# A third buffer for queries and decays, and turns of 13 pieces with the low-rank products in two parts

## The chip, the cores and the metric

The kernel runs on one core of a Trainium2 chip. The metric is the device time of one execution in microseconds. Before the change it is 1311.18 us, the median of three runs (1310.85 to 1312.26).

## What is computed

One encoder layer on 256 tokens of width 2048: a norm, an input projection, three mixers side by side (neighbourhood attention, RWKV-7, retention), an output projection, and an MLP of width 8192. In short:

```
h = rms_norm(x);  z = h @ w_in                     # 2048 -> 7296 columns, 57 tiles of 128
y = concat(attention(z_a), rwkv7(z_b), retention(z_c)) @ w_out
x = x + rms_norm(y)
x = x + rms_norm(square(relu(rms_norm(x) @ w_up)) @ w_down)

# rwkv7: 12 heads of 64, in two directions d (forward, backward)
z = z + mu_prev * (z_prev - z) + mu_next * (z_next - z)
w[d] = w0[d] + tanh(wd[d]) @ w2[d]                 # low rank, 64 -> 768
decay[d] = exp(-exp(-softplus(-w[d]) - 0.5));  a[d] = sigmoid(a0[d] + ad[d] @ a2[d])
kk = k * k_k / norm(k * k_k);  kd[d] = k * (1 + (a[d] - 1) * k_a);  b[d] = kk * a[d]
state = state * decay + (state @ -kk) b^T + v kd^T;  y = state @ r     # per token
y = (group_norm(y) + bonus) * (sigmoid(gd) @ g2)
```

## The kernel before

Every large product is made with weights and activations split into a high and a low fp32r part, so that one depth (128 rows of the contraction for a tile of 128 columns) is three matmuls of 256 tokens: high by high, high by low, low by high. Where a tile is "wide" or the two activation halves are taken at once, fewer and longer ones (512 columns) do the same. Weights arrive by SP's DMAs in half tiles of 8 depths into a ring `raw`; ACT makes the high part (`hi`, L1588), VectorE the low part (`lo`, L955).

The input projection is 57 x 16 = 912 depths, and it is the filler of everything else in the front half of the kernel. The order of the work is written out by hand: every engine runs the same skeleton `stage_a` (L456) with its own functions, and at each `gap()` the engine does what the projection wants of it at this point: TensorE some depths (`DONE`, made by `depths_before`, L106, says how far each gap goes), ACT and VectorE the splits, the drains of finished tiles (`scaled_nr` L999, `by_token`) and the token shifts (`shift_step` L1028) that have come due by depth. There are 42 gaps of 8 depths (the dense stage), then six turns, which share 352 depths evenly, then 12 gaps of the tail, and the attention and retention stage.

RWKV is computed for six pairs of heads t = 0 to 5, in chunks of 64 tokens (NC = 4). A turn t has four jobs at once:

- `products` (4 gaps, `KEY_GAPS`): TensorE multiplies keys by queries for each direction (`key_products`, L2193, into banks 4 and 5), VectorE masks them (`mask_products`, L1140), POOL and VectorE begin the inverse (`first_inverse`, L1151; `first_transposed`, L1078, and `crossed`, L1071), the bonus and the transposed values come (`bonus_and_v`, L2203 and L2208; ACT copies them out at L1750 and L1751, VectorE's `take_bonus` is L1165), the transposed keys (L2228, copied out by ACT at L1755).
- five `level`s of 2 gaps each, which double the inverse of a triangular matrix: TensorE `make_p` (L2258), VectorE `take_p` (L1198, L1202), TensorE `make_q` (L2273, in the last level L2276), VectorE `take_q` (L1213) and the transposes. `make_p` of a level needs `take_q` of the one before, `make_q` needs `take_p` and the transposes. At the end ACT's `take_inverse` (L1768).
- the `chunk` steps of the pair before, t - 1: 12 steps, one at each gap: `g` (L2302, L2328; ACT copies at L1791), `u` (L2337; copied out by ACT at L1795 for the lower half and by VectorE at L1244 for the upper), `state_and_y` (L2356, L2363; new state on VectorE, L1257, L1259).
- the preparation of the next pair, t + 1, in pieces: `feed` (square, root, factor, lora, spread, norm) and `tilde` (decays, keys, queries). They are run at the places `early` (after a gap of the products), `between` (after the first gap of a level, ahead of `make_q`, `take_q`) and `behind` (after its second gap).

Of these pieces: `lora` is the four low-rank products of the pair, w2 and a2 for both directions (L2175). The rows of direction 0 lie in partitions 0 to 63, those of direction 1 in 64 to 127, and `LORA_BANK` sends direction 0 to bank 2 and direction 1 to bank 4. ACT takes them out by four sigmoids (L1692) and `spread` (L2160) puts the key norm's factor over the rows of bank 5. In tilde, VectorE makes `sums` (L1108, L1111; for direction 1 L1113, L1116) and `keys` (L1123, L1124), ACT `key_scales` (L1707), the exponentials `decays` (L1716 to L1718) and `again` (L1728, L1730), POOL the factors of the keys (L762, L768), `queries` (L783, L784) and the bonus (L774). The queries and decays of a pair go to `ar[p]` and `ec[p]` with p = t % 2, so those of pair t + 1 overwrite those of t - 1, whose chunks run in this turn: POOL waits for `y_done` of pair t - 1 first, and the placement is this:

```
early = [(root,), (factor,), (lora, norm), (tl[0],)]
between = [(tl[1],), (), (), (), (tl[4],)]
behind = [(), (), (), tl[2:4], tl[5:7]]
```

where tl[0] is key_scales and the first key factors, tl[1] sums and decays of direction 0, tl[2:4] queries, keys and again of direction 0, tl[4] sums and decays of direction 1, tl[5:7] its queries, keys and again. So the keys of direction 1 are made by VectorE after the last gap of a turn.

## Time and profile before

| | us |
|---|---|
| median of three runs | 1311.18 |
| the profiled execution | 1311.31 |
| its span, first to last instruction | 1309.5 |
| TensorE busy in it | 1286.8 (98%) |
| VectorE busy | 838.7 (64%) |
| ACT busy | 640.4 (49%) |
| POOL busy | 324.1 (25%) |
| mean granted TensorE clock | 0.998 of 2.4 GHz |

Of the span, 2 to 129 us are the dense stage, 129 to 375 us the six turns, 375 to 400 the tail, to some 504 us attention and retention, then the output projection (to about 590), the up projection (to about 950) and the down projection. A share of busy time is a mean over all of these; the rows below look at the turns alone. In the timeline, neighbouring instructions of the same line are merged into one row with their count; the fp32 matmuls of the small products appear as two records each. The end of a matmul is modelled, its start is recorded, so distances between starts are used where tenths of a microsecond matter.

### The profile page before, as it was taken

To read this page: it belongs to the slowest core of one execution; us is meant where nothing else is said; L and a number is where in the kernel's file an instruction comes from. 1 tells how busy PE (TensorE), PEld (TensorE's weight loads), DVE (VectorE), ACT (ScalarE), POOL (GpSimd) and SP (SyncE) were. 2 spreads that over 40 slices of the span, in tenths; PEclk is the share of its full clock that TensorE was granted. 3 is DMA by queue.
4 is the path that set the end of the run, shared out by engine and by line. 5 is a ranking of instruction groups with operands and counts; after the bars stand their busy time and mean duration, and the time that the engine had idled before them with its cause. 6 is when DMAs were issued, how large, how long until landed. Compare 5 with 4: busy or idle time off the path is not lost.

```text
span 1309.5 us, 24352 instructions
## 1 busy us (share of the span) xinstructions
PE 1286.8 (98%) x9986; PEld 1104.1 (84%) x9986; DVE 838.7 (64%) x1162; ACT 640.4 (49%) x979; POOL 324.1 (25%) x266
## 2 busy tenths in 40 slices
PE   8999999999999999999999999999999999999997
PEld 7888888778888898888888888888888888888886
DVE  7778888887877978557555555555555555555565
ACT  6565565556433446446444444444444444444453
POOL 0224343233315220001555555555410000000000
PEclk9999999999999999999999999999999999999999
DMA  9766323332486447745766666666666666666672
GB/s 303 193 179 191 99 82 98 99 99 85 124 154 170 113 129 242 257 145 160 223 186 188 191 191 187 188 191 191 187 191 193 196 193 194 194 194 193 195 234 89
DMA packets 267695, 226.24 MB, mean 173 GB/s; under 512 B 15233, under 2 KB 240641, under 8 KB 266945
## 3 DMA queue, kind: packets, MB, share of 16 engines
q1 hardware_dynamic: 267344, 223.51, 57.4%
q8 instruction: 79, 1.29, 0.4%
q0 software_dynamic: 240, 1.18, 0.2%
q14 instruction: 32, 0.25, 0.1%
HBM read 222.56 MB, written 2.10 MB: 172 GB/s over the span
## 4 chain that ended last, share of the span: by engine, by line
PE 69%; DVE 3%; issue 1%; ACT 1%; DVEq 0%; ACTq 0%
PE psum L2485 33%; PE psum L2031 18%; PE psum L2042 9%; PE psum L2015 2%; PE psum L2021 2%; PE psum L2016 2%; DVE w_lo L955 1%; PE psum L2462 0%; PE psum L2431 0%; ACT w_hi L1588 0%; PE psum L2542 0%; DVE arena L1496 0%; PE psum L2373 0%; PE psum L2453 0%; PE psum L2258 0%
## 5 line engine op out<-in xcount | busy, mean ns | idle before, releaser
L955 DVE TENSOR_TENSOR w_lo<-raw,w_hi 128x1024 fp32r<-128x1024 f32 x393 | 498.9, 1271 | 370.6 <-ACT w_hi L1588 367.3
L1588 ACT ACTIVATE w_hi<-raw 128x1024 fp32r<-128x1024 f32 x393 | 417.0, 1065 | 450.6 <-PE psum L2485 198.3
L2485 PE MATMUL psum<-w_hi,act_both 128*128 128x512 f32 x1216 | 327.6, 389 | 0.9 <-DVE arena L1417 0.9
L2031 PE MATMUL psum<-act_both,w_hi 128*128 128x512 f32 x1296 | 315.4, 392 | 0.0
L2031 PEld LDWEIGHTS psum<-act_both,w_hi 128*128 128x128 f32 x1296 | 237.0, 188 | 45.2 <-issue 0.2
L2485 PEld LDWEIGHTS psum<-w_hi,act_both 128*128 128x128 f32 x1216 | 228.0, 188 | 49.0 <-DVE arena L1417 1.1
L2485 PE MATMUL psum<-w_lo,act_both 128*128 128x512 f32 x608 | 187.6, 389 | 0.0
L2042 PEld LDWEIGHTS psum<-act_both,w_lo 128*128 128x128 f32 x1296 | 169.4, 191 | 7.7
L2042 PE MATMUL psum<-act_both,w_lo 128*128 128x256 f32 x1296 | 173.3, 283 | 0.0
L2485 PEld LDWEIGHTS psum<-w_lo,act_both 128*128 128x128 f32 x608 | 114.1, 188 | 23.9
L900 POOL TENSOR_TENSOR arena<-arena 128x512 f32<-128x512 f32 x32 | 42.4, 1325 | 286.7 <-DVE arena L1529 286.7
L2015 PE MATMUL psum<-act_both,w_hi 128*128 128x256 f32 x416 | 113.1, 304 | 0.0
L2016 PE MATMUL psum<-act_both,w_hi 128*128 128x256 f32 x416 | 104.2, 282 | 0.0
L2015 PEld LDWEIGHTS psum<-act_both,w_hi 128*128 128x128 f32 x416 | 78.8, 189 | 5.6 <-issue 1.2
L2016 PEld LDWEIGHTS psum<-act_both,w_hi 128*128 128x128 f32 x416 | 79.2, 190 | 0.3
L903 POOL TENSOR_SCALAR arena<-arena 128x512 f32<-128x512 f32 x32 | 74.1, 2315 | 2.8
L2021 PE MATMUL psum<-act_both,w_lo 128*128 128x256 f32 x416 | 68.5, 283 | 0.0
L905 POOL TENSOR_TENSOR arena<-arena 128x512 f32<-128x512 f32 x32 | 61.3, 1916 | 2.7
L2021 PEld LDWEIGHTS psum<-act_both,w_lo 128*128 128x128 f32 x416 | 58.0, 191 | 0.2 <-DVE w_lo L955 0.2
L2095 PE MATMUL psum<-w_hi,act_both 128*128 128x512 f32 (+1 forms) x96 | 37.2, 397 | 0.4 <-DVE arena L999 0.2
L802 POOL TENSOR_TENSOR arena<-arena,row_scale 128x512 f32<-128x512 f32 (+1 forms) x11 | 18.2, 1650 | 68.5 <-DVE arena L990 46.2
L2097 PE MATMUL psum<-w_hi,act_both 128*128 128x512 f32 (+1 forms) x96 | 33.4, 357 | 0.0
(252 smaller groups left out, 1250.7 us busy)
## 6 DMA issues: line engine op xcount, KB each, us to landing
raw<-in_w_up SPq DMA_DIRECT2D x128, 512.0 KB, 4.0
raw<-in_w_down SPq DMA_DIRECT2D x128, 512.0 KB, 4.6
raw<-in_w_in SPq DMA_DIRECT2D x113, 512.0 KB, 4.1
raw<-in_w_out SPq DMA_DIRECT2D x32, 512.0 KB, 4.7
arena<-in_na_rpb SPq DMA_DIRECT2D x16, 128.0 KB, 5.2
arena<-in_x SPq DMA_DIRECT2D x2, 1024.0 KB, 7.8
arena<-in_x_t SPq DMA_DIRECT2D x3, 512.0 KB, 7.9
out_x<-arena SPq DMA_DIRECT2D x3, 512.0 KB, 2.7
```

The source lines that it names most:

```text
L900: pool.tensor_tensor(r, r, token_scale.unsqueeze(1).broadcast_to([P, 2, T]), ALU.mult).then_inc(s["up_scaled"], 1)
L903: pool.tensor_scalar(r, r, 0.0, None, ALU.max).then_inc(s["up_scaled"], 1)
L905: pool.tensor_tensor(u[:, 2 * q:2 * q + 2], r, r, ALU.mult).then_inc(s["relu_free"], 1)
L955: dve.tensor_tensor(by_half(h, low(h)), by_pair(h, raw[:, place[h] % RAW]), by_half(h, high(h)).bitcast(F32), ALU.subtract).then_inc(s["lo ...
L1588: act.activation(by_half(h, high(h)), by_pair(h, raw[:, place[h] % RAW]), ACT.Copy).then_inc(s["hi_half"], 1)
L2015: pe.matmul(dst, w_hi[:, h % SPLIT, at:at + P], act_hi[:, kt], start=kt == 0, stop=False)
L2016: pe.matmul(dst, w_hi[:, h % SPLIT, at:at + P], act_lo[:, kt], start=False, stop=False)
L2021: last = pe.matmul(dst, w_lo[:, h % SPLIT, at:at + P], act_hi[:, kt], start=False, stop=kt == KT - 1)
L2031: last = pe.matmul(bank[b], w_hi[:, h % SPLIT, at:at + P], act_both[:, kt].rearrange("p a t -> p (a t)"), start=kt == 0, stop=stop and kt ...
L2042: last = pe.matmul(bank[b][:, 0:T], w_lo[:, h % SPLIT, at:at + P], act_hi[:, kt], start=False, stop=stop and kt == kts[-1])
L2095: pe.matmul(dst, act_lo[:, kt, tokens], w, start=kt == 0 and (t == 0 or count == 4), stop=False, skip_group_check=count != 4)
L2485: last = pe.matmul(bank[4 * t + 2 * j + b], lhs[:, tokens], w[:, b * 512:(b + 1) * 512], start=start, stop=stop)
```

## The change

The pieces of the next pair get new places, the turn has 13 gaps in place of 14, and the queries and decays have three buffers; the third, `EARLY_AR`, lies in the last six tiles of the area that the input projection fills later (`nr`), with a wait in `place_free` for it. Pair t uses buffer `AR_SLOT[t]`. For pairs 1 to 4 (`own_queries`) no pair of the last two turns has the same buffer; pair 5 shares one with pair 3. lora is now `lora_part(0)` and `lora_part(1)`, each with its direction's two products into the two halves of bank 2; spread comes before them and also writes bank 2. In VectorE's products, bonus moves ahead of the first gap and the chunk's step 1 ahead of first_inverse(1).

```diff
-KEY_GAPS = 4
+KEY_GAPS = 3
-        LORA_BANK = [2, 4]
-        kk_wide = bank[5].rearrange("p (a t) -> p a t", a=2)[:, :, P:T]
+        lora_half = [bank[2][:, 0:T], bank[2][:, T:2 * T]]
+        kk_wide = bank[2][:, 0:T].rearrange("p (a t) -> p a t", a=2)
...
+        EARLY_AR = NR_MAIN + MAIN_T * T - 1536
+        AR_TILE = (EARLY_AR - NR_MAIN) // T
+        ar.append(cut(EARLY_AR, 2, NC, 3 * C))
+        ec.append(small[:, 0:8].rearrange("p (d c) -> p d c", d=2))
+        AR_SLOT = [1, 0, 2, 1, 0, 1]
+        def own_queries(t):
+            return not any(AR_SLOT[b] == AR_SLOT[t] for b in (t - 1, t - 2) if b >= 0)
+        def last_in_slot(t):
+            return max((b for b in range(t) if AR_SLOT[b] == AR_SLOT[t]), default=None)
...
-                    square, root, factor, lora, norm = feed(t + 1)
+                    square, root, factor, spread, norm, lora, lora_late = feed(t + 1)
                     tl = tilde(t + 1, 1 - p)
-                    early = [(root,), (factor,), (lora, norm), (tl[0],)]
-                    between = [(tl[1],), (), (), (), (tl[4],)]
-                    behind = [(), (), (), tl[2:4], tl[5:7]]
+                    early = [(root,), (factor,), (spread, norm)]
+                    behind[0] = (lora_late, tl[0])
+                    if own_queries(t + 1):
+                        between = [(lora,), (tl[1],), tl[2:5], tl[5:7], tl[7:9]]
+                    else:
+                        between = [(lora,), (tl[1],), (tl[2],), (tl[5],), (tl[3], tl[4], tl[6])]
+                        behind[4] = tl[7:9]
...
-        PE_STARTS = {20: "root", 23: "lora"}
-        FIRST = {18: "square", 21: "root", 22: "factor", 24: "norm", 25: "lora"}
+        PE_STARTS = {20: "root", 22: "spread", 24: "lora", 25: "lora_late"}
+        FIRST = {18: "square", 21: "root", 22: "factor", 24: "norm", 25: "lora", 26: "lora_late"}
...
+            if AR_TILE <= j + 1 < MAIN_T:
+                eng.wait_ge(s["y_done"], 4 * (AR_SLOT.index(2) + 1))
...
                 def queries(d):
-                    if t >= 2:
-                        pool.wait_ge(s["y_done"], 4 * (t - 1))
-                    a_ = ar[p][:, d]
+                    if last_in_slot(t) is not None:
+                        pool.wait_ge(s["y_done"], 4 * (last_in_slot(t) + 1))
+                    if AR_SLOT[t] == 2:
+                        pool.wait_ge(s["pad_free"], PADS + RW_GROUPS)
+                    a_ = ar[AR_SLOT[t]][:, d]
...
-                return [first, nothing, bonus_and_queries, lambda: key_rate(1), nothing, lambda: queries(1), nothing]
+                return [first, nothing, nothing, bonus_and_queries, lambda: key_rate(1), nothing, nothing, lambda: queries(1),
+                        nothing]
...
-                return [nothing, lambda: sums(0), nothing, lambda: keys(0), lambda: sums(1), nothing, lambda: keys(1)]
+                return [nothing, lambda: sums(0), lambda: keys(0), nothing, nothing, lambda: sums(1), nothing, nothing,
+                        lambda: keys(1)]
...
                 mask_products(0)
+                bonus()
                 steps[0]()
                 gap()
                 run(early[0])
-                bonus()
                 mask_products(1)
+                steps[1]()
                 first_inverse(1)
-                steps[1]()
                 first_transposed(0)
...
+                def lora_part(d):
+                    act.wait_ge(s["lora_done"], 2 * t + d + 1)
+                    for n, (dst, bias_name) in enumerate(((sig_w, "w0"), (rate, "a0"))):
+                        act.activation(dst[:, d], lora_half[n], ACT.Sigmoid,
+                                       bias=vect(bias_name)[:, d * RW_CT + t:d * RW_CT + t + 1]).then_inc(s["lora_free"], 1)
                 def lora():
+                    act.activation(small[:, 241:242], eps, ACT.Sigmoid)
                     act.wait_ge(s["cum_ready"], 5 * t)
                     act.wait_ge(s["kb_ready"], 2 * t)
-                    act.wait_ge(s["lora_done"], t + 1)
-                    for d in (1, 0):
...
+                    lora_part(0)
+                def lora_late():
+                    lora_part(1)
...
-                return [key_scales, lambda: decays(0), nothing, lambda: again(0), lambda: decays(1), nothing,
+                return [key_scales, lambda: decays(0), nothing, nothing, lambda: again(0), nothing, lambda: decays(1), nothing,
                         lambda: again(1)]
...
                 def spread():
+                    pe.wait_ge(s["kk_root"], t + 1)
+                    pe.wait_ge(s["bonus_out"], t)
+                    pe.wait_ge(s["v_taken"], t)
                     pe.wait_ge(s["kk_factor"], t + 1)
...
-                    pe.wait_ge(s["bkt_ready"], 2 * t)
+                    pe.wait_ge(s["kk_ready"], t + 1)
+                    lora_part(0)
+                def lora_part(d):
+                    pe.wait_ge(s["lora_free"], 4 * t + 2 * d)
+                    h = slice(d * C, (d + 1) * C)
                     for n, (w_s, z_s) in enumerate(((w2s, z_wd), (a2s, z_ad))):
-                        for d in range(2):
-                            h = slice(d * C, (d + 1) * C)
-                            last = pe.matmul(bank[LORA_BANK[d]][:, n * T:(n + 1) * T], w_s[h, t * P:(t + 1) * P],
-                                             z_s[h], start=True, stop=True)
+                        last = pe.matmul(lora_half[n], w_s[h, t * P:(t + 1) * P], z_s[h], start=True, stop=True)
                     last.then_inc(s["lora_done"], 1)
-                    spread()
-                return [nothing, kk_sum, nothing, lora, nothing]
+                return [nothing, kk_sum, nothing, spread, nothing, lora, lambda: lora_part(1)]
...
                 pe.wait_ge(s["bkt_ready"], 2 * t + 2)
-                if t < RW_CT - 1:
-                    pe.wait_ge(s["lora_free"], 4 * (t + 1) + 2)
...
-                    if n == 0 and t < RW_CT - 1:
-                        pe.wait_ge(s["kk_ready"], t + 2)
```

## Rows read from the trace of the kernel before

**Rows 1.** The page's shares: engine, busy us, share of the span, instructions.

```profile
PE 1286.8 (98%) x9986; PEld 1104.1 (84%) x9986; DVE 838.7 (64%) x1162; ACT 640.4 (49%) x979; POOL 324.1 (25%) x266
```

**Rows 2.** Windows, one a turn: length, busy us of each engine, clock, DMA.

```profile
129.23:167.50 38.27, 35.91 (x584) 32.23 (x583) 32.26 (x66) 21.60 (x38) 10.76 (x15) 1.00 0.38 110
167.50:209.27 41.77, 41.31 (x755) 37.03 (x755) 35.36 (x76) 23.12 (x50) 14.55 (x20) 1.00 0.31 91
209.27:251.37 42.10, 41.08 (x684) 31.71 (x683) 34.01 (x74) 23.42 (x51) 13.55 (x20) 1.00 0.34 95
251.37:292.85 41.48, 40.74 (x665) 30.56 (x664) 33.46 (x73) 24.54 (x51) 14.61 (x20) 1.00 0.33 98
292.85:334.50 41.65, 41.12 (x722) 34.81 (x721) 32.83 (x73) 24.44 (x51) 14.44 (x20) 1.00 0.32 91
334.50:375.27 40.77, 39.31 (x734) 35.45 (x734) 32.26 (x68) 15.96 (x32) 8.64 (x13) 1.00 0.37 107
```

**Rows 3.** Timeline of TensorE: start, us, line, count [idle before, releaser]; longest waits.

```profile
138.98 0.49 PE L2175 MATMUL psum<-arena 64*128 64x256 f32 x2 [0.44 <-ACT arena_later L1755]
...
148.55 0.66 PE L2258 MATMUL psum<-arena 64*64 64x32 f32 x31 [1.22 <-DVE arena L1213]
...
165.25 0.69 PE L2276 MATMUL psum<-arena 64*64 64x64 f32 x32 [0.48 <-issue]
...
218.65 0.45 PE L2356 MATMUL psum<-arena_later 128*64 128x64 f32 x8 [0.55 <-DVE arena_later L1244]
...
227.13 0.50 PE L2095 MATMUL psum<-w_hi,act_both 128*128 128x512 f32 x1 [0.22 <-DVE arena L999]
...
338.21 1.05 PE L2193 MATMUL psum<-arena_later,arena 64*128 64x128 f32 x14 [0.56 <-DVE arena_later L1140]
```

**Rows 4.** Timeline of TensorE, the low-rank products in turn 2.

```profile
220.53 1.13 PE L2175 MATMUL psum<-arena 64*128 64x256 f32 x8
221.59 0.66 PE L2160 MATMUL psum<-cst,small 128*64 128x128 f32 x8
```

**Rows 5.** Timeline of TensorE, a full-height fp32 product in the tail.

```profile
379.93 1.13 PE L2373 MATMUL psum<-arena 128*128 128x256 f32 x4
380.71 0.47 PE L2015 MATMUL psum<-act_both,w_hi 128*128 128x256 f32 x1
```

**Rows 6.** Timeline of TensorE, one dense piece of 12 records, turn 1.

```profile
195.20 0.39 PE L2015 MATMUL psum<-act_both,w_hi 128*128 128x256 f32 x1
...
196.82 0.67 PE L2273 MATMUL psum<-arena 64*64 64x32 f32 x32
```

**Rows 7.** Timeline of VectorE, front of turn 2.

```profile
209.95 0.80 DVE L1123 SCALAR_TENSOR_TENSOR arena<-arena 128x256 f32<-128x256 f32 x1
210.67 0.95 DVE L1124 TENSOR_TENSOR arena<-arena 128x256 f32<-128x256 f32 x1
211.55 1.28 DVE L1140 TENSOR_TENSOR arena<-psum,cst 128x512 f32<-128x512 f32 x2
...
217.33 0.85 DVE L1151 TENSOR_TENSOR arena<-arena,cst 64x256 f32<-64x256 f32 x2
218.21 0.29 DVE L1244 COPY arena_later<-psum 64x128 f32<-64x128 f32 x1
```

**Rows 8.** Timeline of VectorE, level 0 of turn 0.

```profile
144.06 1.23 DVE L955 TENSOR_TENSOR w_lo<-raw,w_hi 128x1024 fp32r<-128x1024 f32 x1 [0.43 <-ACT w_hi L1588]
145.20 0.96 DVE L1028 SCALAR_TENSOR_TENSOR arena<-arena,vec 128x256 f32<-128x256 f32 x1
146.08 1.22 DVE L1108 TENSOR_TENSOR_SCAN arena<-cst,arena 128x256 f32<-128x256 f32 x1
147.33 0.77 DVE L1111 TENSOR_TENSOR arena<-arena 128x256 f32<-128x256 f32 x1
148.02 0.47 DVE L1213 TENSOR_TENSOR arena<-psum,arena 128x128 f32<-128x128 f32 x2
```

**Rows 9.** Timeline of ACT, products of turn 4.

```profile
301.68 0.38 ACT L1750 ACTIVATE arena_later<-psum 64x256 f32<-64x256 f32 x1
```

More of the change, by code:

```diff
@@ L473, in turn @@
                     if t < RW_CT - 2:
-                        behind[3] = [feed(t + 2)[0]] + behind[3]
+                        behind[3] = [feed(t + 2)[0]]
                 else:
@@ L479, in turn @@
                     level(t, p, n, steps[KEY_GAPS + 2 * n:KEY_GAPS + 2 * n + 2], between[n], behind[n])
-            square, root, factor, lora, norm = feed(0)
+            square, root, factor, spread, norm, lora, lora_late = feed(0)
             tl = tilde(0, 0)
-            named = {"square": (square,), "root": (root,), "factor": (factor,), "lora": (lora,),
-                     "norm": (norm,), "sums_0": tl[0:2], "keys_0": tl[2:4], "sums_1": (tl[4],), "keys_1": tl[5:7]}
+            named = {"square": (square,), "root": (root,), "factor": (factor,), "spread": (spread,), "lora": (lora,), "lora_late": (lora_late,),
+                     "norm": (norm,), "sums_0": tl[0:2], "keys_0": tl[2:5], "sums_1": tl[5:7], "keys_1": tl[7:9]}
             for n in range(DENSE_GAPS):
@@ L755, in feed @@
             def feed(t):
-                return [nothing] * 5
+                return [nothing] * 7
             def tilde(t, p):
@@ L868, in decay_state @@
                         c = n if d == 0 else NC - 1 - n
-                        last = pool.tensor_scalar(state_dec[:, d], state[:, d], ec[q][:, d, c:c + 1], None, ALU.mult)
+                        last = pool.tensor_scalar(state_dec[:, d], state[:, d], ec[AR_SLOT[b]][:, d, c:c + 1], None, ALU.mult)
                     last.then_inc(s["dec_ready"], 1)
@@ L1093, in kk_norm @@
                                              kk_wide, ALU.mult, ALU.mult).then_inc(s["kk_ready"], 1)
-                return [nothing, nothing, kk_factor, nothing, kk_norm]
+                return [nothing, nothing, kk_factor, nothing, kk_norm, nothing, nothing]
             def tilde(t, p):
@@ L1184, in products @@
                 gap()
-                steps[3]()
                 run(early[2])
-                gap()
-                run(early[3])
             def level(t, p, n, steps, between, behind):
@@ L1256, in new_state @@
                         if n == 0:
-                            last = dve.tensor_scalar(state[:, d], new, ec[q][:, d, c:c + 1], None, ALU.mult)
+                            last = dve.tensor_scalar(state[:, d], new, ec[AR_SLOT[b]][:, d, c:c + 1], None, ALU.mult)
                         else:
-                            last = dve.scalar_tensor_tensor(state[:, d], new, ec[q][:, d, c:c + 1], state_dec[:, d],
+                            last = dve.scalar_tensor_tensor(state[:, d], new, ec[AR_SLOT[b]][:, d, c:c + 1], state_dec[:, d],
                                                             ALU.mult, ALU.add)
@@ L1697, in lora @@
                         act.activation(z_gd, z_gd, ACT.Sigmoid)
-                return [square, root, nothing, lora, nothing]
+                return [square, root, nothing, nothing, nothing, lora, lora_late]
             def tilde(t, p):
@@ L1759, in products @@
                 run(early[2])
-                steps[3]()
-                gap()
-                run(early[3])
             def level(t, p, n, steps, between, behind):
@@ L2233, in products @@
                 run(early[2])
-                steps[3]()
-                gap()
-                run(early[3])
                 pe.wait_ge(s["bkt_ready"], 2 * t + 2)
-                if t < RW_CT - 1:
-                    pe.wait_ge(s["lora_free"], 4 * (t + 1) + 2)
             def level(t, p, n, steps, between, behind):
@@ L2327, in g @@
                                 h = slice(e * C, e * C + C)
-                                last = pe.matmul(g_ps[h, at[d]], ar[q][h, d, cd[d], 2 * e * C:2 * e * C + C], state[h, d],
+                                last = pe.matmul(g_ps[h, at[d]], ar[AR_SLOT[b]][h, d, cd[d], 2 * e * C:2 * e * C + C], state[h, d],
                                                  start=False, stop=True, skip_group_check=True)
@@ L2344, in u @@
                                 h, o = slice(e * C, e * C + C), slice((1 - e) * C, (2 - e) * C)
-                                pe.matmul(y_ps[o, at[d]], ar[q][h, d, cd[d], C:2 * C], state[h, d], start=d == 0,
+                                pe.matmul(y_ps[o, at[d]], ar[AR_SLOT[b]][h, d, cd[d], C:2 * C], state[h, d], start=d == 0,
                                           stop=False, skip_group_check=True)
```

24 lines of the change are left out of this document (9 added, 15 removed).

## The prediction

> **What bounds the kernel now.** Read the shares of the engines first: TensorE is busy for 1286.8 of 1309.5 us, VectorE for 64% [rows 1]. So no engine but TensorE can shorten the kernel; what can change is TensorE's own work and the 22.7 us in which it waits. Then the six turns of the RWKV stage, one window each (from a turn's first key product to the next one's) [rows 2]: they are all that the change touches, with the dense stage before them. TensorE idles there for 2.36 + 0.46 + 1.02 + 0.74 + 0.53 + 1.46 = 6.57 us; the other 16 us lie at the start, in attention, at the end. VectorE is the engine that is short in a turn: 32 to 35 us busy of some 41. The waits themselves [rows 3] show who is late: VectorE in nearly all (L1213 take_q, L1140 mask_products, L1244 the upper half of u, L999 a drain), ACT's copies once (L1755).
>
> The idle column understates a wait, since a matmul's modelled tail covers its beginning. Before the 1.22 us of L2258 [rows 3] the last dense matmul started 1.50 us earlier; without a wait this distance is 0.21. The wait costs 1.29. Summed so over all places in the six turns (distance of starts less the distance without a wait) I get 2.8, 0.5, 1.5, 0.6, 1.0 and 1.7 us, together 8.2. This is the most that better order alone can give back.
>
> **Part 1: the low-rank products in two parts (L2165 to L2178).** Before, lora is four matmuls of K = 64, alternating between the lower rows (d = 0) and the upper rows (d = 1) of the array and between two banks. Each fp32 matmul is two records, so there are 8: they take 1.13 us to the modelled end and 1.06 us to the start of L2160 [rows 4]. A full-height product of the same width (L2373, 128 rows, 256 columns) needs 1.13 us for only 4 records [rows 5]. So in lora two half-height records run at once, at 0.21 us per pair. After the change a part holds one d, that is one row half, and both its matmuls need it: 4 records one after the other, 4 x 0.21 + 0.10 at its first record + 0.10 before a tile of another shape = 1.06 us, as long as the whole was. Two parts: 2.12, so +1.06 for each of the six pairs (five in turns 0 to 4, one in the dense stage): +6.4 us. It all lies on TensorE, which nothing covers. Bounds: L2373's slot to the first dense record is 0.78 [rows 5], which would make it 6 x (2 x 0.78 - 1.06) = +3.0; with no overlap of a weight load with the matmul before (0.31 each, the first one's distance) a part is 1.25, and it is +8.6. I take the middle one, because L2175 has the same tile shape and the same neighbours.
>
> The trace has no case of two half-height matmuls in succession on the same rows. The Trainium skill, "TensorE: Matmul & The Clock Gate", section "Why this matters for your kernels", says that small-K matmuls overlap when each lands in a row group of its own, and that one of K = 32 alone takes as long as one of K = 128. By that rule the halves serialize, and it speaks against this change; the trace agrees as far as rows 4 and 5 go.
>
> **Part 2: the first pair, in the dense stage.** lora and spread formed one burst of fp32 work between dense pieces; now spread (gap 22), lora (24) and lora_late (25) are three. Each further burst breaks the dense run once more. Price of a break [rows 6]: from the first record of a dense piece to the next small matmul it is 1.62 us for 12 records, whose starts stand 0.12 apart, 0.18 too much, and the small record before it holds on for 0.10 longer than before another small one: 0.28. Two more bursts: +0.6 us. VectorE's factor is ready a gap before spread is reached, so no wait.
>
> **Part 3: 13 gaps in a turn.** The dense work of the turns is fixed (352 depths, 3 records of 0.12 us each, or fewer and longer ones where tiles are wide); it is cut into 78 pieces of 4.5 depths in place of 84 of 4.2. Six breaks fewer: 6 x 0.28 = -1.7 us (bounds 6 x 0.18 = -1.1, and -2.1 if the small record's hold is 0.16).
>
> **Part 4: where the waits go.** Old and new, site by site:
> - Front of a turn. In turns 1, 2 and 4 VectorE begins with keys(1) of this very pair (0.80 + 0.95 us) ahead of mask_products(0) [rows 7], so key_products(1) waits (0.5, 0.2 and 0.2 us), then the bonus product (0.2) and the first state step (0.6). With a third buffer keys(1) is done in the last level of the turn before, for pairs 1 to 4; bonus goes ahead of the gap and u's upper half (L1244) ahead of first_inverse (0.85 us). -1.7.
> - The last gap of the products is gone, so level 0's make_p comes 1.9 us sooner, and VectorE's queue has to have crossed zt over by then. Take turn 4: key_products end at 294.0, masks and bonus to 295.9, a lo 1.22, then mask_products(1) from the end of key_products(1) at 297.8: 1.27, u 0.29, inverse 0.85, transposed 0.45, a lo 1.22, factor 0.4, to 302.3; take_bonus waits for ACT's four copies (4 x 0.38 [rows 9] after 301.3), to 303.3; crossed 0.89, to 304.2 (durations in [rows 7], or of the same lines in that turn). TensorE gets to spread at 304.45 and to make_p at 305.05. It fits with 0.8 us; no new wait, but this margin is what is late next.
> - Turn 0. lora waits for ACT's copies (0.5), later level 1's make_p for take_q (1.29), behind a lo, a shift and sums(0) at 1.22 + 0.77 [rows 8]. Now VectorE has nothing between level 0's take_p and take_q, while TensorE has lora there. Level 4's make_q waited 0.55 (turn 0) and 0.44 (turn 4) behind keys(0), which moves to level 2. -2.6 of 2.8; 0.2 stays.
> - Level 0: u waits for ACT's g behind the four sigmoids (turn 4, 0.3), make_p for take_q and a drain (turn 3, 0.6); L999 at 227.13 (0.5) falls a gap earlier than TensorE's need by the new depths (drain due from depth 466, bank needed at 472, now in different gaps). -1.2.
> - Turn 5. Its pair shares a buffer with pair 3, so queries(0) still waits for the last y of chunk 3, and ACT now has again(0) (1.0 us) ahead of decays(1). keys(1) is later by 0.3 and key_products(1) waits about 1.0 (0.6 before); the waits behind it, 1.1 us, go as above. -0.7, and 0.2 more at key_products(0).
> - POOL and SP: the queries move earlier, their waits for y_done of an older chunk are long met. The new wait of main tiles 18 to 23 for chunk 2 is met two turns ahead. No DMA is added; SP's wait for chunk 4's end ahead of the bias loads falls in the same gap as the load before it.
> - ACT: the added Sigmoid on one column brings the table load (1.28 us) forward, it adds none; the piece is 0.2 us of an engine half idle.
> Together -6.0 + 0.2 = about -5.9; some 2.3 us of waits are left. Bounds: -8.2 (all go) and -3 (the 13-gap turn brings new ones).
>
> **Sum.** 6.4 + 0.6 - 1.7 - 5.9 = -0.6 us on the profiled execution's 1311.31; the median of the runs is 0.13 lower. 1311.18 - 0.6 = 1310.6.
>
> **Rivals.**
> - *VectorE becomes late in the levels* (slower). sums and keys now stand between take_p and take_q in levels 1 to 4. In turn 0, which has no chunk steps, TensorE needs from the end of make_p to the next one 2 x 1.9 + 0.6 = 4.4 us. VectorE: take_p 0.5, lo 1.22, shift 0.5, sums 1.1, take_q 0.47 = 3.8, but 4.6 with POOL at work beside it (1.22 + 0.77 for the sums [rows 8]). It decides once that queue passes 4.4; 0.2 in each of 20 levels is +4: 1314.6. Against it: a lo falls in only 56% of gaps, and turns 1 to 4 have some 0.6 us more room.
> - *The halves come cheap* (faster). If a part costs 0.78, part 1 is +3.0: 1310.6 - 3.4 = 1307.2. For it: L2373 does it; against: its neighbours have its own tile shape.
> - *The waits are only moved*: TensorE keeps 8.2 us of waits, each with another name: 1316.5. Against it: most of them are a VectorE queue that gets shorter by 1.8 us at the point of need.
> - *A weight load can't overlap on the same rows.* Then a part is 1.25: 1310.6 + 12 x 0.19 = 1312.9. Against it: L2373's records, all on the same rows, follow each other at 0.21. The Trainium skill, same page, section "The mechanism", says that LDWEIGHTS overlaps with matmuls in flight only when the row group differs; by that rule this case would hold, and the trace disagrees for full-height tiles.
>
> **How the numbers follow.** Forecast 0.48; late VectorE 0.13; cheap halves 0.22; moved waits 0.06; no overlap 0.11. What a measurement of this kernel can tell from no change is 0.2%, 2.6 us: under 1308.6 is faster, over 1313.8 slower. Faster: cheap halves (0.20) and the forecast with all waits gone (0.08) = 0.28. Slower: late VectorE 0.10, moved waits 0.05 = 0.15. The range goes from the cheap halves (1307.2) to late VectorE (1314.6) with 0.2 us below the lower, and leaves out moved waits and cheap halves with no waits left (1304.9), some 2 in 10.
>
> **What would show it.** L2175: 24 records in place of 48 in each part's d, each part some 1.06 us to the next small matmul, starts 0.21 apart, none paired. Six breaks fewer. No TensorE wait on L1244 and none at level 4's make_q; one on mask_products in the last turn. The turns' idle sum falls from 6.6 to under 2.5 while TensorE's busy time grows by 4 to 6. Wrong would be: paired starts in lora, or waits for take_q and take_p in levels 1 to 4.

## The result, and where the time is in the profile after

The changed kernel takes 1317.16 us (median; 1314.9 to 1318.21) against 1311.36 for the kernel before on the same chip: ratio 1.0044, 95% interval 1.0033 to 1.0055. It is slower by 0.44%, and the prediction (1310.6 us, "same") was wrong.

Two things have to be told apart. The profiled execution took 1314.9 us, 3.6 more than the profiled one of before; it was the quickest of its five, and the median stands another 2.3 us above it. So I look for 3.6 us in this trace, and for the rest in another execution's. A "stand" below is a stretch in which TensorE waits for another engine.

The shares of the engines in the profiled execution, to be laid beside [rows 1]:

```profile
PE 1290.4 (98%) x9986; PEld 1106.9 (84%) x9986; DVE 836.7 (64%) x1162; ACT 642.6 (49%) x985; POOL 327.0 (25%) x266
```

TensorE is busy for 3.6 us more with the same number of records. Where, the windows say, one a turn as in [rows 2]:

```profile
130.19:169.46 39.27, 36.67 (x585) 32.69 (x584) 32.34 (x67) 22.69 (x44) 12.56 (x17) 1.00 0.38 106
169.46:212.06 42.60, 41.91 (x755) 37.50 (x754) 34.70 (x76) 24.24 (x50) 14.90 (x20) 1.00 0.32 91
212.06:253.37 41.31, 41.31 (x683) 32.24 (x682) 32.56 (x73) 23.73 (x50) 14.88 (x20) 1.00 0.32 92
253.37:296.42 43.05, 41.35 (x664) 31.08 (x664) 32.82 (x72) 24.35 (x51) 15.70 (x20) 1.00 0.31 91
296.42:339.05 42.63, 41.69 (x722) 35.40 (x721) 32.53 (x71) 24.09 (x47) 13.40 (x18) 1.00 0.34 97
339.05:379.03 39.98, 39.07 (x740) 35.47 (x741) 32.18 (x67) 15.88 (x32) 8.82 (x13) 1.00 0.40 115
```

The first turn starts 0.96 us later (130.19 for 129.23). The turns' lengths change by +1.00, +0.83, -0.79, +1.57, +0.98 and -0.79 us. From the first product of L2373's kind in the tail (379.93 before, 383.47 now) both kernels need the same 929.6 us. So the loss is 1.0 in the dense stage and 2.8 in the turns, less 0.2 between the last turn and that product. The dense stage's share is the least certain: the start of the first turn moves by up to 1.1 us between executions of the same dense stage (128.68 to 129.74 in the four traces with the old one, 130.19 to 130.74 in six with the new one).

Only turn 2 looks as forecast: it has no idle time left (41.31 busy of 41.31). Over all six, TensorE's idle column sums to 6.84 us, and it was 6.57. Who is waited for, from the waits of TensorE over the turns (line waited at, releaser: us in total, times, longest):

```profile
PE psum L2125 <- DVE w_lo L978: 1.7, 1, 1.7
PE psum L2276 <- DVE arena L1234: 1.4, 2, 0.7
PE psum L2294 <- issue: 1.3, 2, 0.9
PE psum L2291 <- DVE arena L1219: 1.1, 2, 0.8
PE psum L2276 <- DVE arena L1094: 0.6, 2, 0.3
PE psum L2218 <- DVE arena_later L1164: 0.6, 1, 0.6
```

The names are other ones than in [rows 3]: the waits for u (L1265, formerly L1244) and for ACT's copies are gone. Four of the rows now lie in the levels, the last one at the front of turn 5. The first is one that no part of the prediction had: a dense matmul that waits 1.67 us for VectorE's low part of a weight half.

The low-rank products in two parts, TensorE in turn 1, to be laid beside [rows 4]:

```profile
183.86 1.13 PE L2202 MATMUL psum<-arena 64*128 64x256 f32 x4
184.92 0.67 PE L2291 MATMUL psum<-arena 64*64 64x32 f32 x32
```

Four records take 1.13 us, and 1.06 to the next start: this is what the prediction said, and it holds for all twelve parts.

### The profile page after: what moved, and what is told of

Read it like the earlier page. It is cut to its first block, busy times and chain, and to the rows that moved or that the text cites. A ratio compares the mean times of both kernels' runs of the same rounds, so it can differ in the third digit from the quotient of the medians.

```text
span 1313.1 us, 24365 instructions
## 1 busy us (share of the span) xinstructions
PE 1290.4 (98%) x9986; PEld 1106.9 (84%) x9986; DVE 836.7 (64%) x1162; ACT 642.6 (49%) x985; POOL 327.0 (25%) x266
## 3 DMA queue, kind: packets, MB, share of 16 engines
q0 software_dynamic: 240, 1.18, 0.3%
## 4 chain that ended last, share of the span: by engine, by line
PE 69%; DVE 3%; issue 1%; ACT 1%; POOL 0%; DVEq 0%; ACTq 0%
PE psum L2503 33%; PE psum L2054 18%; PE psum L2065 9%; PE psum L2038 2%; PE psum L2044 2%; PE psum L2039 2%; DVE w_lo L978 1%; PE psum L2480 0%; PE psum L2449 0%; PE psum L2560 0%; DVE arena L1517 0%; PE psum L2391 0%; PE psum L2276 0%; PE psum L2471 0%; PE psum L2439 0%
```

## The stand in turn 3, and what the clock does behind it

The changed kernel around 272 us: one row of ACT, then the timeline of VectorE, then TensorE.

```profile
266.19 1.06 ACT L1609 ACTIVATE w_hi<-raw 128x1024 fp32r<-128x1024 f32 x1
```

```profile
266.12 0.48 DVE L1219 TENSOR_TENSOR arena<-psum,cst 128x128 f32<-128x128 f32 x2
269.37 0.49 DVE L1234 TENSOR_TENSOR arena<-psum,arena 128x128 f32<-128x128 f32 x2 [2.77 <-PE psum L2291]
269.89 0.29 DVE L1265 COPY arena_later<-psum 64x128 f32<-64x128 f32 x1
270.21 0.45 DVE L1101 STREAM_TRANSPOSE arena<-arena 128x256 f32<-128x256 f32 x1
270.69 0.89 DVE L1094 STREAM_TRANSPOSE arena<-arena 64x256 f32<-64x256 f32 x2
271.61 1.22 DVE L978 TENSOR_TENSOR w_lo<-raw,w_hi 128x1024 fp32r<-128x1024 f32 x1
```

```profile
272.89 0.51 PE L2125 MATMUL psum<-w_lo,act_both 128*128 128x512 f32 x1 [1.67 <-DVE w_lo L978]
273.33 1.13 PE L2202 MATMUL psum<-arena 64*128 64x256 f32 x4
```

Read it from the bottom. The dense matmul wants w_lo, which VectorE makes from 271.61 to 272.83. Its input w_hi was there at 267.25, and VectorE had nothing to do for 2.77 us up to 269.37, 2.1 of them with w_hi ready; but in its order of work this low part stands behind level one's take_q, u and transposes, in the next gap. A late conversion here is not a busy engine, it is a place in a list.

The list is made by depths. Half h is wanted from depth 8h on; ACT rounds it in the first gap that begins at 8h - 14 or later, VectorE makes its low part from 8h - 11. Half 67 belongs to a group four tiles wide in which the order of slots is swapped at the start, so it is wanted at 532, not 536. Before, turn 3's gaps begin at 512, 516, 520, 524, 528, 532: the low part (525) comes in the fifth, the use in the sixth. With 13 pieces they begin at 512, 516, 520, 524, 530, 534: both fall into the fifth. I had checked such a boundary for one drain (part 4 names it) and for no weight half.

Now the same place in a second execution of the same kernel, whose mean clock was .997 where the first had .999. Windows, the seventh figure is the granted clock:

```profile
273.50:275.00 1.50, 1.50 (x7) 0.86 (x8) 0.00 (x0) 0.00 (x0) 0.00 (x0) 1.00 0.39 42
275.00:276.00 1.00, 1.00 (x35) 0.94 (x36) 0.01 (x1) 0.84 (x2) 0.00 (x0) 0.58 0.72 264
276.00:277.00 1.00, 1.00 (x17) 0.88 (x17) 0.84 (x4) 0.95 (x2) 0.20 (x1) 0.50 0.53 197
277.00:278.00 1.00, 1.00 (x5) 0.81 (x4) 1.00 (x2) 0.98 (x3) 1.00 (x2) 0.50 0.07 12
278.00:279.00 1.00, 1.00 (x5) 0.76 (x3) 1.00 (x2) 0.65 (x1) 1.00 (x1) 0.72 0.01 4
```

TensorE stood for the same 1.67 us and went on at 273.50 at full clock; from about 275.2 to 278.6 the grant is 0.50, the lower level (1.2 GHz). Laid side by side, this execution is 0.6 us behind the first up to the stand (273.50 for 272.89), and 1.8 at the next turn's first key product (298.24 for 296.42): the spell costs 1.2 us.

## Experiments

All were timed against the kernel before on the same chip (its medians: 1310.89, 1310.65, 1310.55 and 1310.62 us in the four groups).

**The changed kernel again.**

> The changed kernel as it is, a second time. Its median stands 5.8 us above that of the kernel before, while the two profiled executions differ by 3.6 us only. If the difference lies in fixed work and waits, this execution has the rows of the first one (dense stage +1.0, the six turns +2.6) and the clock .999, and 1315 to 1318 us. If a spell at the lower clock level makes the rest, the slower executions show a mean granted clock of .995 to .997 and one more stretch at half clock, 2 to 3 us long in cost, outside the last 10 us of the span.

1316.41 us, ratio 1.0042 (1.003 to 1.0055); the profile is the one above. Of ten executions of the changed kernel two have the clock .999 and take 1314.65 and 1314.9 us; eight have .995 to .997 and take 1316.2 to 1318.2. The kernel before has .998 or .999 in every one. So the slower executions have lost clock, as the second theory says. What the one profile shows is a single spell, worth 1.2 us. The executions at .995 and .996 are slower still (1317.2 to 1318.2); no trace shows what they had, so of the 2.3 us between the first profile and the median only about half is seen in rows.

**Half 67 one gap earlier** (called the early half below).

```
+        def reached_half(h, lag, early):
+            return HALF_KT * (h - SPLIT + 1) + (early if h == EARLY_HALF else lag)
+        EARLY_HALF = 67
-  while ... HALF_KT * (at["lo"] - SPLIT + 1) + LO_LAG <= reached(at["gap"]):
+  while ... reached_half(at["lo"], LO_LAG, 4) <= reached(at["gap"]):
-  while ... HALF_KT * (at["hi"] - SPLIT + 1) + HI_LAG <= reached(at["gap"]):
+  while ... reached_half(at["hi"], HI_LAG, 0) <= reached(at["gap"]):
```

> The changed kernel with one thing moved: weight half 67 is rounded and its low part formed one gap earlier (ScalarE and VectorE; only that half). In both profiled executions of the changed kernel TensorE stood 1.67 us there for VectorE's low part, in turn 3, and in the second one its granted clock was at half for some 3 us right after, which cost another 1.5 us. If that stand is also what brings the spell at the lower clock, the profile gains 1.6 us and the median 3 or more: 1313 to 1314.5, with a clock of .998 or .999 in nearly all executions. If the spell has nothing to do with the stand, only the 1.6 go: 1315 to 1316, clocks as before (.995 to .999).

1312.68 us (1312.3 to 1313.41), ratio 1.0016 (1.0007 to 1.0026); clocks .998 and .999 throughout. Turn 3 of its profile:

```profile
253.43:294.51 41.08, 41.05 (x665) 31.08 (x664) 32.74 (x72) 24.44 (x51) 15.68 (x20) 1.00 0.32 96
```

It is 1.97 us shorter, turns 0, 1, 2 and 4 stay as long as they were within 0.03, and the executions no longer spread; the median even lies a little under the first theory's range. Against the kernel before, +5.5 (or +5.8) has become +2.0: the one conversion in the wrong gap cost 3.5 to 3.8 us. 2.0 of it are the stand; the rest went together with the low mean clocks.

**A stand put into the kernel before.**

```
+        def lo_lag(h):
+            return 10 if h == 67 else LO_LAG
-  ... + LO_LAG <= reached(at["gap"])      (VectorE alone)
+  ... + lo_lag(at["lo"]) <= reached(at["gap"])
```

> The kernel before, with one conversion moved the other way: VectorE forms the low part of weight half 67 one gap later, in the gap whose dense piece uses it, so that TensorE has to stand for it in turn 3, some 1 to 2 us. If a stand of that length there is what the clock answers with a spell at the lower level, the median rises by more than the stand, to 1313 to 1315, the executions spread over some 3 us, and their mean clocks reach from .999 down to .996. If the spell belongs to something else in the changed kernel (its halves, its prepared pairs), the median rises by the stand alone, 1311.7 to 1312.7, with clocks of .998 and .999.

1313.79 us, ratio 1.0025 (1.0015 to 1.0035): +3.2 us. TensorE's row at the stand, and the windows behind it:

```profile
273.59 0.73 PE L2105 MATMUL psum<-w_lo,act_both 128*128 128x512 f32 x2 [2.24 <-DVE w_lo L958]
```

```profile
275.00:276.00 1.00, 1.00 (x9) 0.78 (x6) 1.00 (x3) 0.28 (x1) 0.00 (x0) 0.70 0.68 236
276.00:277.00 1.00, 1.00 (x4) 0.81 (x3) 0.58 (x1) 0.00 (x0) 0.00 (x0) 0.50 0.60 229
277.00:278.00 1.00, 1.00 (x14) 0.35 (x15) 0.00 (x0) 0.00 (x0) 0.00 (x0) 0.50 0.63 47
278.00:279.00 1.00, 1.00 (x50) 1.00 (x47) 0.17 (x1) 0.00 (x0) 0.00 (x0) 0.59 0.65 227
```

Nothing of the change is in this kernel, and it has the same spell, some 3.4 us at half clock in both (each slice's shortfall from 1.00, over 0.50, summed), beginning 1.7 to 1.8 us behind the stand's end. So a stand at this place is enough to bring it. It does not come every time. Only the two traces above show the spell itself; for the other executions there is the mean clock, and .998 and .999 are what undisturbed ones have too. By that, with a stand of 2.24 us six of the eight executions had it (.997, 1313.7 to 1315.2 us) and two had not (.998, 1312.4 and 1312.7). With 1.67 us it was eight of the ten of the changed kernel and four of the five with the first sums early (below), with 1.4 us (two banks, below) two of eleven, at .997. The two kernels with turn 0's old places (below) have a stand of 1.27 us at the front of turn 1, and two of eleven each lie at .996 or .997 and 1.5 to 2 us higher. The kernel before, with 1.22 us in turn 0 [rows 3], never did, and neither did the one with 1.3 us in turn 0 (third buffer alone, below). So these lengths overlap, and length alone does not decide it.

**The second part's products left out** (on top of the early half).

```
-                return [nothing, kk_sum, nothing, spread, nothing, lora, lambda: lora_part(1)]
+                def left_out():
+                    pe.wait_ge(s["lora_free"], 4 * t + 2)
+                    pe.sem_inc(s["lora_done"], 1)
+                return [nothing, kk_sum, nothing, spread, nothing, lora, left_out]
```

> The kernel with half 67 early, with the second low-rank part's two products left out (ScalarE reads the first part's values again, so the second direction's rates are not computed; all waits stay). If each part's 1.06 us lies on the path: six parts, 6.3 us less, 1306.3. If VectorE sets the pace in turn 0, the part there comes back as a wait: 5.3 us less, 1307.4. If parts are mostly hidden: over 1310.

1306.55 us, ratio 0.9968 (0.9955 to 0.998). That is 6.1 us under the 1312.68, for 6 x 1.06 = 6.4: the parts lie on the path with nearly their full length. It also prices the rest of the change: without the second part and the late half, the kernel is 4.0 us under the one before (1310.55).

**The kernel before with its four products in another order.**

```
-                    for n, (w_s, z_s) in enumerate(((w2s, z_wd), (a2s, z_ad))):
-                        for d in range(2):
-                            h = slice(d * C, (d + 1) * C)
+                    for d in range(2):
+                        h = slice(d * C, (d + 1) * C)
+                        for n, (w_s, z_s) in enumerate(((w2s, z_wd), (a2s, z_ad))):
```

> The kernel before, with only the order of the four low-rank products changed: both products of direction 0 (the same rows of the array) and then both of direction 1, so that two neighbours no longer lie on different row halves all the time. Same matmuls, banks, waits and places. If two products on the same rows follow one another only at the end of the first (my reading of the two parts of 1.06 us), the burst takes 1.7 to 2.1 us for 1.13, in six turns: +3.6 to +5.9 us, 1315 to 1317. If the burst is hidden or the order of rows is no matter: 1311.4, within 0.5 of before.

1310.8 us, ratio 0.9999 (0.999 to 1.0008): nothing, as the second theory said; my reading, the first one, was wrong. TensorE in turn 2, first only the records that start before 220.3, then the whole burst:

```profile
220.10 0.49 PE L2175 MATMUL psum<-arena 64*128 64x256 f32 x2
...
220.10 1.14 PE L2175 MATMUL psum<-arena 64*128 64x256 f32 x8
```

Two records start within 0.01 us of each other though the program now issues both products of the lower rows first. In the changed kernel the same stretch holds one record (a part uses one row half):

```profile
183.86 0.48 PE L2202 MATMUL psum<-arena 64*128 64x256 f32 x1
```

The records don't name their rows; I read each pair as one record of either half, since records of one half start 0.21 us or more apart in the changed kernel. So what serialises is how much work each row half has, not the order in the program. Four products on two halves (1.06 us before, 1.08 here, to the next start) and two products on one (1.06) take the same time. The Trainium skill, "TensorE: Matmul & The Clock Gate", section "The mechanism", says that matmuls start and end strictly in program order; by this reading the rows don't agree, for tiles on different row halves.

**One burst again, over two banks** (changed kernel; direction 1 into bank 3, which lies idle between the first state and the second u).

```
+        def lora_bank(t):
+            return [2, 3] if t else [2, 4]
+                    for n, (w_s, z_s) in enumerate(((w2s, z_wd), (a2s, z_ad))):
+                        for d in range(2):
+                            last = pe.matmul(bank[lora_bank(t)[d]][:, n * T:(n + 1) * T], ...)
+  u:  if n == 0 and b == 0 or n == 1 and b + 2 < RW_CT:
+          pe.wait_ge(s["lora_free"], 4 * (b + 1 + n) + 2)
```

> The changed kernel with its low-rank products in one burst again, direction 0 into bank 2 and direction 1 into bank 3 (free between the first state's drain and the second chunk's u), at the place of its first half; the second half's place stays empty. If the serialised halves are the main cost: six times (2.11 less 1.13) = 5.9 us less, 1311 to 1312, up to 1313.5 if u of level one waits for ScalarE's first two sigmoids. If they are hidden and VectorE in the levels sets the time: 1316.5 to 1317.5.

1310.52 us, ratio 0.9997 (0.9988 to 1.0005): 5.9 us under the changed kernel. By rows: the six bursts give back 6.4, u's four stands cost 4 x 0.7 (the distance of starts is 1.18 us here, 0.48 without a stand), and the low mean clocks are nearly gone. Its rows in turn 1 (8 records in the time of 4, then u stands for the sigmoids), and its waits:

```profile
182.07 1.14 PE L2207 MATMUL psum<-arena 64*128 64x256 f32 x8
183.14 0.67 PE L2297 MATMUL psum<-arena 64*64 64x32 f32 x32
184.32 0.27 PE L2363 MATMUL psum<-arena 64*64 64x64 f32 x2 [0.51 <-ACT arena L1714]
```

```profile
PE psum L2363 <- ACT arena L1714: 2.1, 4, 0.5
PE psum L2128 <- DVE w_lo L981: 1.4, 1, 1.4
```

**Third buffer and spread preparation alone** (kernel before: 14 pieces, low-rank burst in its old place; sums, keys and queries in levels two to five).

```
-                    between = [(tl[1],), (), (), (), (tl[4],)]
-                    behind = [(), (), (), tl[2:4], tl[5:7]]
+                    if own_queries(t + 1):
+                        between = [(tl[1],), (), tl[2:5], tl[5:7], tl[7:9]]
+                    else:
+                        between = [(tl[1],), (), (tl[2],), (tl[5],), (tl[3], tl[4], tl[6])]
+                        behind[4] = tl[7:9]
```

> The kernel before (14 pieces, the four low-rank products in one burst over two banks at their old place) with only the third buffer for queries and decays and the preparation of the next pair spread over levels two to five. If the low-rank halves are what made the changed kernel slow and the rest of the change is worth a little, the waits at the front of turns 1 to 4 (0.46 to 1.02 us each) go and nothing is paid: 1307.5 to 1310. If keys and sums in the levels cost as much there as they cost at the front (VectorE late with the next operand), it stays at 1311 to 1313.

1311.41 us, ratio 1.0005 (0.9996 to 1.0014). Nothing is gained. The fronts of turns 1 to 4 are all but free of waits, as forecast (0.2 us at one low-rank burst), and the waits are elsewhere: 1.8 us at the last product of the levels, 0.9 at key_products(1).

```profile
PE psum L2299 <- issue: 1.8, 3, 1.3
PE psum L2281 <- DVE arena L1236: 1.2, 1, 1.2
PE psum L2216 <- DVE arena_later L1163: 0.9, 1, 0.9
```

Most of it is in turn 0, which is as long here as in the changed kernel (39.27), though it has neither the 13 pieces nor the two parts. So the new places of the preparation are what lengthens it, by 1.0 us:

```profile
128.68:167.90 39.22, 35.93 (x583) 32.22 (x582) 33.62 (x68) 23.21 (x43) 12.23 (x17) 1.00 0.36 104
```

**The first sums behind level one, ahead of the key scales** (changed kernel).

```
-                    behind[0] = (lora_late, tl[0])
+                    behind[0] = (lora_late, tl[1], tl[0])
-                        between = [(lora,), (tl[1],), tl[2:5], ...
+                        between = [(lora,), (), tl[2:5], ...
```

> The changed kernel with the first direction's decay sums and exponentials run behind level one, ahead of the key scales, and no longer between the two takes of level two. The sums then don't run beside GpSimd's key products (scan 0.68 for 1.22 us, difference 0.43 for 0.78) and not ahead of VectorE's take of q. If VectorE's place and its slowing beside GpSimd hold TensorE up in the levels: 0.8 us less in turn 0, 0.9 in turn 4, up to 0.6 elsewhere, 1314.5 to 1316. If in turn 0 VectorE is simply full (no idle time from 148 to 168 us), the waits move to the next level and it stays at 1316.5 to 1317.5.

1317.75 us, ratio 1.0057 (1.0044 to 1.0069). The scan is quick now (0.69 at 316.56 in turn 4), and it doesn't help: ACT has the exponentials and key scales ahead of its g, and TensorE stands 0.3 to 1.3 us at g in four turns.

```profile
PE psum L2346 <- ACT arena L1827: 3.6, 4, 1.3
```

**Turn 0's token shifts narrowed** (early half; 4 columns for 256 in the last two groups).

```
-                last = dve.scalar_tensor_tensor(z, zpad[..., 2 * late:2 * late + T], ..., z, ...)
+                last = dve.scalar_tensor_tensor(z[:, 0:4], zpad[..., 2 * late:2 * late + 4], ..., z[:, 0:4], ...)
```

> The kernel with half 67 early, with the token shifts of the last two groups (a VectorE operation of 0.41 to 0.95 us in each level of turn 0 and some of turn 1) narrowed to 4 columns, which leaves most of the shift out. If VectorE without idle time is what holds TensorE in turn 0 (stands of 0.80, 0.71 and 1.00 us there), they shrink by what the shifts took, 2 us or more in all: 1310 to 1310.8. If the stands come from single late operands in a row of their own (the sums' place), half of them stay: 1311.5 to 1312.7.

1312.01 us, ratio 1.0009 (1.0000 to 1.0018): 0.7 less, in the second theory's range. The intervals of the two kernels overlap, but the profiles agree on the place: turn 0 is 0.8 us shorter than with the early half alone (39.27) and turn 1 as long (42.60 there).

```profile
130.28:168.72 38.44, 36.62 (x584) 32.70 (x583) 30.98 (x67) 22.69 (x44) 13.44 (x17) 1.00 0.38 106
168.72:211.34 42.62, 41.91 (x754) 37.51 (x753) 34.47 (x76) 24.26 (x50) 14.91 (x20) 1.00 0.32 91
```

One of turn 0's three long stands went (0.80); these stay:

```profile
PE psum L2299 <- issue: 0.9, 1, 0.9
PE psum L2281 <- DVE arena L1239: 0.6, 1, 0.6
```

**Turn 0's preparation back at its old places** (early half).

```
+                    if t == 0:
+                        between = [(lora,), (tl[1],), (), (), tl[5:7]]
+                        behind[3], behind[4] = tl[2:5], tl[7:9]
```

> The kernel with half 67 early, with the preparation of the next pair put back to its old places in turn 0 alone: bonus, keys and queries of direction 0 behind level four, the second sums in level five, the rest behind it. If having it in levels two to five is what leaves the stands of 0.71 and 1.00 us at the end of turn 0, they go, and what comes back is the stand of 0.5 us at the front of turn 1: 1.2 us less, 1311.5. If these stands belong to the level chain itself in turn 0, which has VectorE's shifts and low parts in it, nothing is gained: 1312.7 to 1313.5.

1312.78 us, ratio 1.0016 (1.0008 to 1.0025), no gain. Two of the eleven executions took 1314.3 and 1314.4 us at a mean clock of .997, the other nine at most 1313.1. Its turns 0 and 1 show why, with the row at the front of turn 1:

```profile
130.40:168.19 37.79, 36.62 (x584) 32.71 (x583) 31.88 (x65) 20.98 (x38) 11.11 (x15) 1.00 0.40 111
168.19:212.12 43.93, 41.99 (x755) 37.51 (x755) 35.51 (x78) 25.92 (x56) 16.31 (x22) 1.00 0.30 86
```

```profile
173.31 0.38 PE L2226 MATMUL psum<-arena 64*128 64x128 f32 x2 [1.27 <-DVE arena_later L1172]
```

Turn 0 is 1.5 us shorter than with the early half alone (39.27), and turn 1 is 1.3 longer (42.60); turn 2 starts at 212.12 in both. The first theory was right on what makes the stands, wrong on what removing them is worth.

**Versions made from this.** "Ahead" is the two-bank kernel with three edits: half 67 early, the sigmoid table loaded in the products' last gap, and the burst ahead of level one's dense piece:

```
                 run(steps[:1])
+                if n == 0:
+                    run(between)
                 gap()
+                if n:
+                    run(between)
                 make_q()
```

> The two-bank version (one low-rank burst in banks 2 and 3) with three edits: the burst ahead of level one's first dense piece instead of behind it, the sigmoid table loaded in the products' last gap, and weight half 67 converted one gap earlier. In the two-bank version TensorE stood 0.51 to 0.7 us for ScalarE's sigmoids before u in four turns (2.1 to 2.8 us) and 1.4 us for half 67. If these stands end the step they are in, all of it is gained: 1306 to 1307.5. If VectorE takes over what they free (it is busy without a break in most of turn 0), 1308.5 to 1310.

1308.65 us, ratio 0.9985 (0.9976 to 0.9994). The stands at u are gone; the burst now stands for the normalised keys, which share bank 2 (2.8 us in three turns). The second theory was the nearer one.

"Ahead" with the sums early, as above:

> The version before this one, with the first direction's sums and exponentials also behind level one, ahead of the key scales. By the theory that VectorE's order in the levels costs: another 1 to 2 us less, 1305 to 1306.5. By the theory that the waits only move: the same as without, within 0.5 us.

1308.52 us, ratio 0.9985 (0.9976 to 0.9994): the same.

"Mixed": ahead only in the turns without that stand.

```
+                ahead = n == 0 and t in (1, 4)
```

> The version with the burst ahead of level one's dense piece, but in turns 0, 2 and 3 behind that piece again, where TensorE had stood 0.79, 1.14 and 0.93 us for VectorE's normalised keys (they share bank 2 with the burst); behind it u stood 0.70 us for the sigmoids in turns 2 and 3 and nothing in turn 0. By those stands 1.5 us less, 1307.2; if the stands only move, 1308.3 to 1309.

1307.65 us (1307.2 to 1308.28), ratio 0.9978 (0.9969 to 0.9987). Here the first theory was the nearer one. It beats both kernels: 2.9 us under before, about 9 under the change. "Mixed" with turn 0's old places:

> The same put-back of turn 0 in the best version so far (one low-rank burst in two banks, ahead of the dense piece in turns 1 and 4 alone, half 67 early). By the first theory 1306.5, by the second 1307.7 to 1308.5.

1308.16 us, ratio 0.9982 (0.9973 to 0.9991): the second theory again.

## Why the prediction was wrong, by its own steps

- *Part 1, the two halves (+6.4): right.* Each part takes 1.06 us; without the second one the kernel is 6.1 us quicker. The Trainium skill, "TensorE: Matmul & The Clock Gate", section "The mechanism", lets a weight load overlap matmuls in flight only on other row groups in one sentence, and in another one also where the load goes to the background weight buffer. By the first one a part would be 1.25 by the prediction's estimate, and the rows say 1.06, so this rival fell. "Cheap halves" (0.78) fell as well.
- *Part 2, the first pair (+0.6): probably too much.* One pair of executions cannot price it: the dense stage grew by 0.96 us in the two profiled ones, by 1.24 between the means of the four and six traces named above. One part is 1.06 of it, so the two further bursts cost 0.2 at most by these, which is within the scatter.
- *Part 3, six gaps fewer (-1.7): its own saving was not measured alone.* Turn 2, the only one without idle time, fits it: 42.10 less its old waits (1.5) is 40.6; plus 1.06 less 0.28 is 41.4; it has 41.31. But the step missed the other thing that fewer pieces do: they shift where the depths of a piece begin, and so which gap a weight half is wanted in.
- *Part 4, the waits (8.2 to 2.3, -5.9): this step failed.* (Its items add up to -6.0, not -5.9.) Summed as the prediction does, by distances of starts, the six turns still hold about 8 us, so it gained 0.2 us. By its items: the front of turns 1 to 4 came as forecast (one of 0.18 is left), turn 5 too (1.7 to 1.05). Turn 0 was to lose 2.6 and lost nothing (0.38, 0.79, 0.71 and 0.99 us now). Turn 3 got the late half, 1.95 with what follows. And 2.0 us of new ones stand in the levels of turns 1, 3 and 4, the longest 0.90 at make_q in turn 4 for take_p. I compared VectorE's queue with TensorE's need in one level; the last two stands of turn 0 come later, at both products of level five. In the rows ahead of them, VectorE makes the second sums just before level four's take_q, then ACT has the exponentials before a weight half, and VectorE waits for that half before it comes to take_p. That this order makes them is shown by turn 0's old places, where both go (0.13 us is left of them).
- *The sum.* Over the turns of the profiled execution: five second parts +5.3, six gaps fewer -1.7, waits -0.2 make 3.4; measured are 2.8, and no run says where the other 0.6 are. By medians, which take in the clock, from run to run: the second parts cost 6.1, the late half 3.5 to 3.8 (a stand and the clock behind it, for which the prediction had no term), and the rest of the change gives back 4.0 where 0.6 - 1.7 - 5.9 = -7.0 were forecast.
- *The rivals.* "The waits are only moved" had 0.06 and said 8.2 us of waits, where there are 8. The waits of turn 0 were moved, as the spread preparation alone (1311.41 for 1310.89) and turn 0's old places show. That its time of 1316.5 is also the median is luck: it holds part 2's 0.6 and no clock, and the execution without a spell took 1314.9; and a quarter of its 8 us are the late half, which is a new stand and not a moved one. "VectorE late in the levels" is what the rows name (L1219, L1234), at half its price.

What stays open: which of VectorE's, ACT's and TensorE's common steps makes the length of turns 0 and 1 together. Two arrangements of the same work gave the same 81.7 to 81.9 us. Taking work out (the shifts, 1.6 us of VectorE's time in the two turns) gave 81.1, so half of that counted; what the other half was hidden behind was not tried.

## What to carry to other kernels

Cutting fixed work into fewer pieces moves every piece's boundary. List, for each operand made just in time, the gap in which it is made and the gap in which it is first used, before and after; one that is made in the gap of its first use is likely to be a stand. Take a wait out of a sum only when the releaser's work is taken out; where it is moved, book the wait at the next place at which the same engines meet, until a trace shows otherwise. Price a stand of TensorE above its length when the median and the profiled execution differ, and look at the mean clock of every execution for that.

## What the runs showed of the hardware

- Behind a stand of 1.67 or 2.24 us in turn 3, TensorE went on at full clock for 1.7 to 1.8 us and then had half clock (1.2 GHz) for some 3.4 us, which cost 1.2 us more in the execution that could be laid beside an undisturbed one. It came in some executions of one kernel and not in others.
- Two row halves of the array each take their own products in turn: with both products of the lower half first in the program, two records still started within 0.01 us of each other, and the burst of 8 records took 1.14 us (1.13 before).
- VectorE's scan over 128 x 256 took 1.22 us where GpSimd worked beside it all through (150.82 us in the changed kernel) and 0.68 where it did not work (161.58); in the kernel with the first sums early, all its scans in the turns took 0.68 to 0.69.
